# Four wide products with unread results ahead of each unit's transposition in the first layer

## The reference, cut to what matters

```python
def attend(q, k, v):
    s = jnp.einsum('btgrd,blgd->bgrtl', q, k, preferred_element_type=jnp.float32) * (ATTN_HEAD_DIM ** -0.5)
    p = jax.nn.softmax(s, axis=-1)
    return jnp.einsum('bgrtl,blgd->btgrd', p.astype(v.dtype), v)
...
    y_attn = blocked_attention(ql, k_all, v_all) * jax.nn.silu(a_g)
...
    if not need_ctx:
        return x_new, ctx
...
    yc_attn = attend(qc.reshape(B, L, ATTN_KV_HEADS, ATTN_Q_PER_KV, ATTN_HEAD_DIM), kc, vc)
```

## Time and profile before

| | us |
|---|---|
| three timed runs, median | 1471.01 |
| lowest and highest of them | 1470.66, 1472.67 |
| the profiled execution, own time | 1467.76 |
| its span in the profile | 1466.0 |

### The profile page before, as it was taken

How to read it: one execution, slowest core, us unless ns; L and a number is a source line. 1 busy time by engine, 2 the same in 40 slices (tenths; PEclk the granted TensorE clock), 3 DMA queues, 4 the chain that set the end, 5 groups by cost and what they waited for, 6 DMA issues and landing times. The chain is left out here.

```text
span 1466.0 us, 19469 instructions
## 1 busy us (share of the span) xinstructions
PE 1352.9 (92%) x8018; PEld 1028.2 (70%) x8018; DVE 650.2 (44%) x1197; ACT 505.0 (34%) x840; POOL 44.6 (3%) x36
## 2 busy tenths in 40 slices
PE   6999897688999999998998979999999989999996
PEld 2787576466678888887975658999776656666663
DVE  2322364777223434457736784566622342222222
ACT  2224431434352323234453546444135221111112
POOL 0000000211000000002000020000000000000000
PEclk7999999889899999999999999999999999999998
DMA  9422210213512234322431201565233558999990
GB/s 388 193 86 87 86 58 29 105 69 115 230 58 87 87 106 181 109 85 101 150 140 58 86 2 59 177 226 175 101 115 115 243 230 336 410 406 403 422 377 31
DMA packets 34223, 238.98 MB, mean 163 GB/s; under 512 B 4304, under 2 KB 4432, under 8 KB 6224
## 3 DMA queue, kind: packets, MB, share of 16 engines
q1 hardware_dynamic: 34128, 237.66, 42.1%
HBM read 236.59 MB, written 1.05 MB: 162 GB/s over the span
## 5 line engine op out<-in xcount | busy, mean ns | idle before, releaser
L229 DVE TENSOR_TENSOR pieces_lo<-weight_ring,pieces_hi 128x1024 fp32r<-128x1024 f32 x154 | 187.5, 1223 | 319.5 <-ACT pieces_hi L221 319.4
L247 PE MATMUL proj<-h_hi,pieces_hi 128*128 128x512 f32 (+1 forms) x816 | 287.2, 352 | 8.3 <-DVE h_lo L1127 2.9
L249 PE MATMUL proj<-h_hi,pieces_lo 128*128 128x512 f32 (+1 forms) x816 | 282.3, 346 | 0.0
L248 PE MATMUL proj<-h_lo,pieces_hi 128*128 128x512 f32 (+1 forms) x816 | 281.3, 345 | 0.0
L221 ACT ACTIVATE pieces_hi<-weight_ring 128x1024 fp32r<-128x1024 f32 x158 | 165.7, 1053 | 132.9 <-PE proj L249 69.2
L247 PEld LDWEIGHTS proj<-h_hi,pieces_hi 128*128 128x128 f32 x816 | 154.2, 189 | 36.6 <-issue 8.7
L248 PEld LDWEIGHTS proj<-h_lo,pieces_hi 128*128 128x128 f32 x816 | 154.9, 190 | 21.7 <-issue 1.4
L249 PEld LDWEIGHTS proj<-h_hi,pieces_lo 128*128 128x128 f32 x816 | 154.2, 189 | 20.5
L1917 PE MATMUL turn<-expert_parts,e_gathered 128*64 128x256 f32 x768 | 85.3, 379 | 0.8 <-DVE e_gathered L2106 0.8
L1917 PEld LDWEIGHTS turn<-expert_parts,e_gathered 128*64 128x64 f32 x768 | 56.0, 137 | 32.4 <-issue 7.3
L761 PE MATMUL turn<-l_diag,l_probs 128*128 128x128 f32 x320 | 48.7, 309 | 29.6 <-DVE l_diag L1191 14.3
(11 more groups left out here) (433 smaller groups left out, 1998.3 us busy)
## 6 DMA issues: line engine op xcount, KB each, us to landing
weight_ring<-in_stream SPq DMA_DIRECT2D x110, 1024.0 KB, 4.8
expert_parts<-in_experts SPq DMA_DIRECT2D x70, 1024.0 KB, 10.9
weight_ring<-in_experts SPq DMA_DIRECT2D x26, 1024.0 KB, 10.7
l_rows<-in_rows SPq DMA_DIRECT2D x2, 768.0 KB, 15.6
l_y_attn<-in_ada_first SPq DMA_DIRECT2D x1, 1024.0 KB, 5.0
l_y_gla<-in_ada_first SPq DMA_DIRECT2D x1, 1024.0 KB, 7.1
l_y_sgu<-in_ada_first SPq DMA_DIRECT2D x1, 1024.0 KB, 8.0
l_q<-in_ada_first SPq DMA_DIRECT2D x1, 1024.0 KB, 9.8
```

What stands on the lines that cost most here:

```text
L229: eng.tensor_tensor(self.part(self.lo_ring[:, n % NPIECE, :], kind), self.raw(slot, c, kind), self.part(self.hi_ring[:, n % NPIECE, :], ki ...
L247: pe.matmul(out, sh, mh, start=start, stop=False)
L248: pe.matmul(out, sh, ml, start=False, stop=False)
L249: return pe.matmul(out, sl, mh, start=False, stop=stop)
```

## The change

In layer 0 only, and for the first head of each unit only, PE issues four products of 128 by 128 with 128 by 512 elements (`h_hi` with itself) into the `turn` bank that the unit's transposition will overwrite. They need the bank but not the probabilities. So that they can stand ahead of the wait for `probs`, the bank is now opened before that wait, in both heads and in both layers.

```diff
                     for u in range(2):
+                        acc = PT.open(pe, J("turn", i, u))
+                        if l == 0 and u == 0:
+                            keep_busy(pe, acc, HH[:, 0, :], 512, 4)
                         pe.wait_ge(*sig.probs.at(2 * i + u + 1))
-                        acc = PT.open(pe, J("turn", i, u))
                         for b in range(2 * (s + 1)):
```

## The result

| | before | after |
|---|---|---|
| median of 11 runs each, us | 1470.66 | 1474.35 |
| lowest to highest, us | 1468.32 to 1472.67 | 1469.85 to 1479.18 |
| ratio, 95% interval | | 1.0028 (1.0016 to 1.0040) |

The change makes the kernel slower by 3.7 us by the medians, where 4.4 us had been forecast. A second series of 12 runs gave 1474.33 against 1470.55 us, ratio 1.0025 (1.0014 to 1.0036). One execution of one kernel further down took 4819.98 us at a mean granted clock of 0.275; it is left out of every number here.

What follows compares the result with a forecast made beforehand. PE sets the pace behind the attention stage; inside it a ring of PE, DVE and ACT binds. Terms 4 x 0.92 + 0.2 + 0.5 = 4.4 us on 1471.0 gave 1475.4 us, range 1469.5 to 1479.5.

Steps and rivals of the forecast that it cites:

- The price of four: Four wide products on PE start 0.229 us apart, so they cost 0.92 us at full clock, 1.72 at half.
- Unit 1: PE's 7.89 us wait is for the bank, so the products come after it; paid: 0.92 us.
- rival C: Products meet a low clock after unit 1 and at units 7, 13, 15: 8.5 us, 1479.5; chance 0.14.
- Units 2, 4, 5, 8, 9, 11, 12, hidden: Unit 2's cost vanishes in an `ada` product's 4.08 us wait; the others run inside waits for the diagonal: cost 0.
- Units 6 and 14, hidden: The second head waits 2.63 and 3.35 us for an `ada` bank that ACT frees independently: cost 0.
- Unit 7: Lies in the half-clock stretch from 291 to 300 us: taken as 0, up to 0.8 at half clock.
- Units 3 and 10: Partly paid: 0.2 us at unit 3 after ACT's lateness, about 0.5 at unit 10 into DVE's chain.
- The sum: Attention stage: four full prices of 0.92 plus 0.2 and 0.5, 4.4 us slower.
- I expect most of the low clock to stay: Half-clock stretches behind units 6 and 14, worth about 2.8 and 4.4 us, would mostly remain.
- Its argument on unit 6: Full clock at 280 to 287 ends the `ada` product about 1.4 us sooner, so the gap stays as long.
- rival A: One half-clock stretch, behind unit 6 or 14, is saved: 1.6 or 0 us, 1471.0 to 1472.6; chance 0.28, shared with no visible effect.
- B: Both half-clock stretches, behind units 6 and 14, are saved: -2.8 us, 1468.2; chance 0.08.

Runs made afterwards that it cites:

- products only where unhidden: Four wide products only in units 0, 1, 3, 7, 10, 13 and 15, where no wait was forecast to hide them, against the kernel before: 1475.84 against 1469.85 us.

## Why the prediction was right, point by point

The stage can be cut at marks that stand in every trace. How much later each piece made the end, against the trace of before; the piece ends at the mark whose start times are given (before, change, its second trace, products only where unhidden). The first piece starts at unit 0's first product (212.72, 214.06, 216.08, 213.05):

| piece, and the mark that ends it | forecast | change | second trace | unhidden only |
|---|---|---|---|---|
| unit 0, to unit 1's first product (245.67, 247.90, 249.91, 246.86) | 0.92 | 0.89 | 0.88 | 0.86 |
| unit 1, to the `ada` product behind unit 2 (259.97, 262.83, 265.80, 261.80) | 0.92 | 0.63 | 1.59 | 0.64 |
| units 3 to 6, to unit 6's second head (290.73, 293.27, 296.63, 293.68) | 0.2 | -0.32 | 0.07 | 1.12 |
| units 7 and 8, to unit 9's transposition (314.32, 316.48, 321.12, 316.89) | 0 | -0.38 | 0.90 | -0.38 |
| units 10 to 12, to the `ada` product behind unit 12 (345.48, 348.12, 352.78, 349.63) | 0.5 | 0.48 | 0.50 | 1.58 |
| unit 13, to the next `ada` product (356.74, 360.33, 364.97, 361.83) | 0.92 | 0.95 | 0.93 | 0.94 |
| unit 14, to unit 15's first product (373.76, 376.28, 380.86, 377.55) | 0 | -1.07 | -1.13 | -1.30 |
| unit 15, to the first projection (385.54, 388.97, 393.57, 390.25) | 0.92 | 0.91 | 0.93 | 0.92 |
| sum | 4.4 | 2.1 | 4.7 | 4.4 |

**The price of four** was 0.92 us by the row of the existing `keep_busy`. Units 0, 13 and 15 show it, 0.86 to 0.95 us in all three traces. Right, and sixteen products ahead of units 13 and 15 cost four times as much each. The 131 ns for such a product, which the Trainium skill, "TensorE: Matmul & The Clock Gate", section "Back-to-back issue gap", gives for a sustained stream, would have made it 0.52 us; it does not hold here.

**The other pieces** scatter by up to 1 us around their terms. They do so without any product too: in the kernel with products only at units 13 and 15, unit 1's piece is 0.97 us longer than before, that of units 3 to 6 0.48 longer, that of units 7 and 8 0.55 shorter and that of units 10 to 12 1.03 longer. The half clock lies at other places in each of these traces. So single traces confirm three of the four full prices and cannot size the small terms.

**Unit 1**, paid in full behind the wait for the keys' bank. The wait is there, 7.8 us, with L255 at its end. The piece was 0.63, 1.59 and 0.64 us, around the 0.92. Whether the 1.59 is rival C's mechanism (the restart at half clock lasting longer) or this scatter is not shown, and no row gives that rival's 3.4 us.

**Units 2, 4, 5, 8, 9, 11, 12, hidden**: the waits for the diagonal shrank from 8.4 to 3.3 us, and the products placed in waits alone had cost 0.08 us by unit 14. Right. **Units 6 and 14, hidden**: their price is nothing by the same run. **Unit 7** was taken at nothing, up to 0.8 at half clock. In the second trace its products ran at half clock (1.88 us up to the transposition) and the piece cost 0.90; in the other two it cost nothing. **Units 3 and 10**, 0.2 and 0.5, were not tried alone.

**The sum**, 4.4 us, lies close to the timed 3.7 and 3.8 us, and in part this is luck. Four full prices of 0.92 are the bulk of it; three of them were measured as forecast, that of unit 1 only within the scatter. Around them errors cancel: what units 1, 3, 7 and 10 cost beyond their terms or short of them in one trace or another, and about 1.1 us won behind unit 14, which the forecast did not have.

**The clock.** "I expect most of the low clock to stay" held on the average over executions: some 10 us less at half clock by their mean clocks, of about 45 in the stage in the trace of before. The first trace of the change, at 22 us less, was an exception. Its argument on unit 6, that the wide products keep the clock up at 280 to 287, so that the `ada` product ends sooner and the gap stays, has the gap right and the cause wrong. PE there in the first trace of the change:

```profile
286.76 1.93 PE L692 MATMUL turn<-weight_ring,silu_c 128*32 128x512 f32 x16 [1.59 <-ACT l_probs_t L1025]
293.27 0.71 PE L763 MATMUL turn<-l_diag,l_probs 128*128 128x128 f32 x4 [3.02 <-ACT l_y_gla L918]
```

And in the kernel with no products:

```profile
286.87 1.93 PE L692 MATMUL turn<-weight_ring,silu_c 128*32 128x512 f32 x16 [1.59 <-ACT l_probs_t L1023]
...
293.38 1.22 PE L761 MATMUL turn<-l_diag,l_probs 128*128 128x128 f32 x4 [3.45 <-ACT l_y_gla L916]
```

The `ada` product runs at full clock in 1.93 us in both, where the trace of before had 3.3: it was the trace of before that had half clock there, as few of the other traces have. The gap of 2.63 us was short for the same reason, and the wide products made 3.02 of the more usual 3.45.

**Behind unit 14** the gap came out as forecast, 2.34 us for 2.4, and the clock fell in it all the same in both traces of the change (0.62 from 366 to 375 in the first, 0.66 from 370 to 380 in the second). Its length can be read off from unit 14's second head to the L702 behind it. Without products there it is 9.74 to 9.77 us in four traces, 8.54 in one and 8.66 in another; with four wide ones 8.76 and 8.70 in the change and 5.54 once, at full clock throughout; with eight 7.11; with ten 7.18 twice. So more products save more of it, but for four the 1.1 us of the change is no more than two kernels without any had. It is rival A's mechanism, in part and not in every execution.

**What the profile was to show**: the first projection 4 to 5 us later. It is 3.4 us later in the first trace and 8.0 in the second, because 1.3 and 3.4 us of it arise before unit 0. The sign should have been the stage's length, not a time from the span's start; but at 2.1 and 4.7 us more, a single trace would not have decided by that either. DVE's L1263 at unit 13 waits 3.54 and 3.53 us, 0.9 longer than 2.61, as said. The transposition still waits for the diagonal at units 5 and 9, no more at unit 4, whose wait of 1.22 us the products fill.

**The rivals.** B, both stretches saved and faster than before: it did not happen with the change, since the paid units are in it. The kernels with products only in gaps live from its mechanism, at 1.9 and 2.4 us of the 7.2 that it put on both stretches. C did not come to 8.5 us.

The Trainium skill, "TensorE: Matmul & The Clock Gate", section "What's actually happening", says that activity releases the throttle. A PE that the profile records as busy is not enough for that here: in the kernel with narrow products in the unhidden units it was busy 10.88 of 11.00 us, and the clock was at 0.69.

## What to carry to other kernels

A filler product is free only if its buffer comes free before the wait that it is to fill ends; where the wait is for that buffer, it lands behind the gap and is paid in full. Put fillers at the few gaps after which PE alone sets the pace, as many as fit (ten in a wait of 3.35 us), and none at places without a wait. The gain to hope for is small: 1.9 to 2.4 of 1470 us here. Count what the clock gives back only up to the next wait for another engine.

## What the runs showed of the hardware that was not expected

- Seven products of 2 columns take 0.80 us of PE's queue and cost 11.4 us over seven units, while four products of 512 columns take 1.04 us and cost 6.0 us in the same units. PE is recorded as busy in both, and the clock over the stage is 0.86 and 0.90.
- The same code reached unit 0 at 212.72, 214.06 and 216.08 us in three traces, and the changed kernel's times spread over 9.3 us (1469.85 to 1479.18). The products do not cause this spread: the kernel without any spreads over 8.3 us (1466.99 to 1475.28) and the one before over 6.8 in 23 runs. Where low-clock stretches fall differs from one execution to the next, so single traces of this kernel should be compared stage by stage, and against a second trace of a kernel without the change.
- Sixteen products that began at half clock, ahead of other work, took 5.57 us and delayed that work by 3.9 us, near the 3.7 us of their price at full clock: the transposition behind them ran in 1.05 us, where without them it had taken 2.05.
